# Further passes of the expert stage run as a pair's, on the weights that pass 11 left, and the pair that needs one changes places with pair 11

## The reference

```python
h = jax.nn.silu(jnp.einsum('td,edf->tef', xf, w_gate)) * jnp.einsum('td,edf->tef', xf, w_up)
h = h * gates.astype(h.dtype)[..., None]      # zero for all but the two chosen experts
y = jnp.einsum('tef,efd->td', h, w_down)
```

## Time and profile before

| what | us |
|---|---|
| median of three runs (622.78 to 623.87) | 623.35 |
| the profiled execution | 622.29 |
| its span, first instruction to last | 620.5 |
| PE busy in the span | 591.4 (95%) |
| VectorE busy | 321.1 (52%) |
| ScalarE busy | 232.6 (37%) |
| GpSimd busy | 53.0 (9%) |
| mean rate of all transfers | 259 GB/s |

### The profile page before, as it was taken

How to read it: one execution, slowest core, us unless ns; L and a number is a source line. 1 busy time by engine, 2 the same in 40 slices (tenths; PEclk the granted TensorE clock), 3 DMA queues, 4 the chain that set the end, 5 groups by cost and what they waited for, 6 DMA issues and landing times.

```text
span 620.5 us, 8828 instructions
## 1 busy us (share of the span) xinstructions
PE 591.4 (95%) x2860; PEld 352.3 (57%) x2860; DVE 321.1 (52%) x702; ACT 232.6 (37%) x413; POOL 53.0 (9%) x126
## 2 busy tenths in 40 slices
PE   7999999999999999999999989999999988988895
PEld 4876796777768677777566743433333333333331
DVE  4649787767767676776665876112111212211137
ACT  6451417375574747547364331111211121111124
POOL 1200001000000000000000012212121211121000
PEclk9999999999999999999999999999999999999999
DMA  8332319922222322221499879999999999999995
GB/s 318 128 135 88 118 34 359 387 77 76 74 69 101 109 68 76 76 84 52 178 343 419 306 274 376 412 419 419 417 420 419 423 418 421 420 417 422 413 386 211
DMA packets 34842, 160.78 MB, mean 259 GB/s; under 512 B 6528, under 2 KB 6912, under 8 KB 23040
## 3 DMA queue, kind: packets, MB, share of 16 engines
q1 hardware_dynamic: 29200, 149.66, 61.5%
q0 software_dynamic: 5472, 10.63, 4.6%
q10 hardware_dynamic: 144, 0.15, 0.1%
HBM read 155.01 MB, written 14.17 MB: 273 GB/s over the span
## 4 chain that ended last, share of the span: by engine, by line
PE 68%; SPq 11%; DMA 9%; DVE 6%; ACT 3%; issue 2%; DVEq 0%; ACTq 0%; POOLq 0%
PE ps L1617 14%; PE ps L1619 13%; PE ps L1618 13%; SPq L564 10%; PE ps L2026 10%; PE ps L2056 5%; DMA wslot<-in_wmoe 5%; PE ps L1758 2%; PE ps L1793 2%; DMA raw<-in_wmix 2%; DVE x L1570 1%; DMA ytok<-yo,idx 1%; PE ps L1740 1%; DMA gy<-ytok 1%; PE ps L1784 1%
## 5 line engine op out<-in xcount | busy, mean ns | idle before, releaser
L2026 PE MATMUL ps<-wslot,xgT 128*64 128x512 f32 x512 | 118.0, 594 | 7.8 <-DMA wslot<-in_wmoe 7.3
L1617 PE MATMUL ps<-xh,wh 128*128 128x512 f32 x256 | 102.5, 400 | 0.0
L1619 PE MATMUL ps<-xl,wh 128*128 128x512 f32 x256 | 99.9, 390 | 0.0
L1618 PE MATMUL ps<-xh,wl 128*128 128x512 f32 x256 | 99.9, 390 | 0.0
L757 ACT ACTIVATE wh<-raw 128x1024 fp32r<-128x1024 f32 x48 | 50.7, 1058 | 119.0 <-PE ps L1619 100.6
L2026 PEld LDWEIGHTS ps<-wslot,xgT 128*64 128x64 f32 x512 | 38.7, 137 | 82.0 <-issue 81.3
L1010 DVE TENSOR_TENSOR wl<-raw,wh 128x1024 fp32r<-128x1024 f32 x48 | 58.6, 1222 | 23.1 <-ACT wh L757 21.8
L2056 PE MATMUL ps<-wslot,hT 128*64 128x512 f32 x264 | 62.3, 598 | 4.2 <-ACT hT L968 2.2
L1523 DVE SCALAR_TENSOR_TENSOR hm<-ps,rt,hs 128x128 f32<-128x128 f32 x24 | 7.3, 345 | 112.9 <-ACT hs L965 112.9
L1617 PEld LDWEIGHTS ps<-xh,wh 128*128 128x128 f32 x256 | 48.1, 188 | 16.1 <-issue 6.7
L1619 PEld LDWEIGHTS ps<-xl,wh 128*128 128x128 f32 x256 | 48.1, 188 | 10.6
(11 more groups left out here) (356 smaller groups left out, 832.1 us busy)
## 6 DMA issues: line engine op xcount, KB each, us to landing
wslot<-in_wmoe SPq DMA_DIRECT2D x91, 1024.0 KB, 19.9
raw<-in_wmix SPq DMA_DIRECT2D x56, 512.0 KB, 4.0
wslot<-in_wmoe SPq DMA_DIRECT2D x8, 512.0 KB, 23.9
gy<-ytok SPq DMA_DIRECT2D x8, 512.0 KB, 10.3
xt<-in_x SPq DMA_DIRECT2D x4, 512.0 KB, 7.8
x<-in_x SPq DMA_DIRECT2D x4, 512.0 KB, 4.5
xnd<-x SPq DMA_DIRECT2D x4, 512.0 KB, 9.5
wslot<-in_wmoe SPq DMA_DIRECT2D x8, 256.0 KB, 4.8
```

The lines of the kernel that those rows point to most:

```text
L1617: pe.matmul(out, sh, mh_, start=start, stop=False)
L1618: pe.matmul(out, sl, mh_, start=False, stop=False)
L1619: return pe.matmul(out, sh, ml_, start=False, stop=stop)
L2026: l = pe.matmul(ps[CAP * s:CAP * s + CAP, 2, :], xgT[:, c, CAP * s:CAP * s + CAP], first_at[s * 4 + c] if first_at and c < 4 else wslot[q] ...
```

## The change

It does four things.

1. **A further pass is a pair's.** VectorE counts further passes by pair (the fuller expert decides), and the pass runs both halves (`pair(m + HEAD, 2, ...)`).
2. **It uses the weights in slot 2.** Pass 11's slot is slot 2 (KEPT = 11), and the first further pass needs no load if pass 11 was that pair's. If more than one is needed, or the pair could not be exchanged, the pair is loaded into slot 2.
3. **The pair that needs the first further pass (the last such pair, if it lies in 7 to 14, SWAP) changes places with pair 11.** VectorE writes the order of the pairs into nxi, SP reads from it which pair to load for passes 7 to 11 and places 12 to 14, and VectorE exchanges the columns of idx and rt (`swap_columns`); GpSimd and ScalarE wait for that (`swapped`).
4. **The slots behind it shift:** pairs 12, 13, 14, 15 use slots 0, 1, 2, 0. So gy, nf and junk3 move to where slot 1 lies, and yf to where slot 2 lies.

Of the diff, the parts that carry this:

```diff
+KEPT = HEAD - 1
+SWAP = range(7, PAIRS - 1)
+N_EXTRA, N_ORDER = 1, 1 + EXTRA
+N_NEED, N_COUNT, N_KEPT = N_ORDER + PAIRS, N_ORDER + PAIRS + 1, N_ORDER + PAIRS + 2
...
-    yf = at("yf", 122 * K, [P, TILES, D])
-
-    gy = at("gy", 48 * K, [P, 2, TILES, D])
-    nf = at("nf", 88 * K, [P, D])
-    junk3 = at("junk3", 92 * K, [P, D])
+    yf = at("yf", 48 * K, [P, TILES, D])
+
+    gy = at("gy", 98 * K, [P, 2, TILES, D])
+    nf = at("nf", 138 * K, [P, D])
+    junk3 = at("junk3", 142 * K, [P, D])
...
-            refill(1, 5, 14)
-            refill(2, 6, 16)
-            for q in range(3):
-                refill(q, 7 + q, 18 + 2 * q)
-
             e.wait_ge(nx_ready, 1)
             nx = e.value_load(nxi[0:1, 0:1], min_val=0, max_val=EXTRA)
 
+            def order(p):
+
+                return e.value_load(nxi[0:1, N_ORDER + p:N_ORDER + p + 1], min_val=0, max_val=NE - 2)
+
+            for p in range(7, 14):
+                refill(p % 3, p - 2, order(p))
+
             def further(count, m):
-                ex = e.value_load(nxi[0:1, bass.ds(m + 1, 1)], min_val=0, max_val=NE - 1)
-                for part, used in enumerate((gu_half, gu_mm, pair_mm)):
-                    lo, hi = PARTS[part]
-                    e.wait_ge(used, count)
-                    e.sem_inc(held, 1)
-                    e.dma_start(wslot[0][0][:, lo:hi], wmoe[bass.ds(ex, 1), :, lo:hi].rearrange(
-                        "a p c -> (a p) c")).then_inc(part_in[part][0][0], 16)
-
-            with e.If(nx > 0):
-                further(HEAD - 2, 0)
-            refill(1, HEAD - 1, 2 * HEAD)
-            refill(2, HEAD, 2 * HEAD + 2)
+
+                refill(2, count, e.value_load(nxi[0:1, bass.ds(m + N_EXTRA, 1)], min_val=0, max_val=NE - 2))
+
+            need = e.value_load(nxi[0:1, N_NEED:N_NEED + 1], min_val=0, max_val=1)
+            with e.If(need > 0):
+                further(HEAD, 0)
             with e.If(nx > 1):
                 with e.Fori(1, nx) as m:
                     further(m + HEAD, m)
-            refill(0, nx + HEAD, 2 * HEAD + 4)
+            refill(2, nx + HEAD, order(14))
...
-            with g.Fori(0, HEAD - 2) as G:
-                g.wait_ge(xgT_mm, FIRST + G + 2)
-                g.sem_inc(held, 1)
-                gather(idx, bass.ds(G + 2, 1), G + 2)
-                scatter(idx, bass.ds(G, 1), G + 1)
+            def rows_of_passes(a, b):
...
+            rows_of_passes(0, SWAP[0] - 2)
+            g.wait_ge(swapped, 1)
+            rows_of_passes(SWAP[0] - 2, HEAD - 2)
...
-            with a.Fori(1, HEAD) as G:
+            with a.Fori(1, SWAP[0]) as G:
+                expert_pass(G, rt[:, bass.ds(G, 1)])
+            a.wait_ge(swapped, 1)
+            with a.Fori(SWAP[0], HEAD) as G:
                 expert_pass(G, rt[:, bass.ds(G, 1)])
...
+                per = ps[:, TOTB, 0:NE].rearrange("p (e h) -> p e h", h=2)
...
+                own.then(d.reduce_max(most, per, axis=AX))
+                own.then(d.tensor_tensor(c8[:, 0:PAIRS, :], bc(most, nck), row(caps[:], PAIRS), ALU.is_gt))
+                own.then(d.reduce_sum(n, c8[:, 0:PAIRS, :], axis=AX))
+                own.then(d.tensor_tensor_scan(upto, ones[:, 0:PAIRS], n, 0.0, ALU.mult, ALU.add))
+                own.then(d.tensor_scalar(above, upto, -1.0, xcnt[:, 0, NE - 1:NE], ALU.mult, ALU.add))
...
+                own.then(d.tensor_scalar(one(0), pair1, float(SWAP[0] + 1), None, ALU.is_ge))
+                own.then(d.scalar_tensor_tensor(out=one(1), in0=pair1, scalar=float(SWAP[-1] + 1), in1=one(0), op0=ALU.is_le, op1=ALU.mult))
...
+                d.scalar_tensor_tensor(out=nxi[0:1, N_NEED:N_NEED + 1], in0=xcnt[0:1, 0, NE - 1:NE], scalar=1.0, in1=one(1),
+                                       op0=ALU.is_ge, op1=ALU.subtract)
...
+                own.then(d.tensor_tensor(moved, moved, iota[0:1, 0:PAIRS], ALU.add))
+                d.tensor_scalar(nxi[0:1, N_ORDER:N_ORDER + PAIRS], moved, 2.0, None, ALU.mult).then_inc(nx_ready, 1)
...
+            def swap_columns():
+
+                d.wait_ge(nx_ready, 1)
+                kept = d.value_load(nxi[0:1, N_KEPT:N_KEPT + 1], min_val=SWAP[0], max_val=SWAP[-1])
+                d.tensor_copy(turn[:, 0:2], idx[:, :, KEPT])
+                own.then(d.tensor_copy(turn[:, 2:3], rt[:, KEPT:KEPT + 1]))
+                d.tensor_copy(idx[:, :, KEPT:KEPT + 1], idx[:, :, bass.ds(kept, 1)])
+                own.then(d.tensor_copy(rt[:, KEPT:KEPT + 1], rt[:, bass.ds(kept, 1)]))
+                d.tensor_copy(idx[:, :, bass.ds(kept, 1)], turn[:, 0:2].rearrange("p (y a) -> p y a", a=1))
+                own.then(d.tensor_copy(rt[:, bass.ds(kept, 1)], turn[:, 2:3]))
+                d.sem_inc(swapped, 1)
...
             rows_T(2)
+            swap_columns()
             nx = extra_columns()
...
+            kept_in = pe.value_load(nxi[0:1, N_COUNT:N_COUNT + 1], min_val=use - 16, max_val=use)
             with pe.If(nx > 0):
                 with pe.Fori(0, nx) as m:
-                    pair(m + HEAD, 0, (m * 16 + use,), True, (m * 16 + (use - 16),))
-            pair(nx + HEAD, 1, (use, use), True)
-            pair(nx + (HEAD + 1), 2, (use, use), True)
+                    pair(m + HEAD, 2, (m * 16 + kept_in,) * 2, True)
+            pair(nx + HEAD, 0, (use, use), True, (use - 16, use - 16))
+            pair(nx + (HEAD + 1), 1, (use, use), True)
             pe.wait_ge(wlast_ready, 1)
             last_terms(0, ident[:], x1[:, 0, :], True, False)
-            pair(nx + (HEAD + 2), 0, (nx * 16 + use, use), True, (nx * 16 + (use - 16), use - 16))
-            pair(nx + (HEAD + 3), 1, (use + 16, use + 16), False)
+            pair(nx + (HEAD + 2), 2, (nx * 16 + kept_in,) * 2, True)
+            pair(nx + (HEAD + 3), 0, (use + 16, use + 16), False, (use, use))
```

More of the change, by code:

```diff
@@ L264, in build @@
     coly = small("coly", [P, 1], U32)
-    nxi = small("nxi", [1, 1 + EXTRA], I32)
+    nxi = small("nxi", [1, N_KEPT + 1], I32)
     warm = small("warm", [P, 1])
@@ L372, in build @@
         extra_ready = sem("extra_ready")
+        swapped = sem("swapped")
         colg_copied = sem("colg_copied")
@@ L726, in _ @@
             gather(idx, slice(1, 2), 1)
-            with g.Fori(0, HEAD - 2) as G:
-                g.wait_ge(xgT_mm, FIRST + G + 2)
-                g.sem_inc(held, 1)
-                gather(idx, bass.ds(G + 2, 1), G + 2)
-                scatter(idx, bass.ds(G, 1), G + 1)
+            def rows_of_passes(a, b):
+                with g.Fori(a, b) as G:
+                    g.wait_ge(xgT_mm, FIRST + G + 2)
+                    g.sem_inc(held, 1)
+                    gather(idx, bass.ds(G + 2, 1), G + 2)
+                    scatter(idx, bass.ds(G, 1), G + 1)
+            rows_of_passes(0, SWAP[0] - 2)
+            g.wait_ge(swapped, 1)
+            rows_of_passes(SWAP[0] - 2, HEAD - 2)
             g.wait_ge(extra_ready, 1)
@@ L1452, in extra_counts @@
                 d.wait_ge(total_mm, 1)
[L1453 to L1461, removed]
+                per = ps[:, TOTB, 0:NE].rearrange("p (e h) -> p e h", h=2)
+                most, n, upto, above = xcnt[:, 0, 0:PAIRS], xcnt[:, 1, 0:PAIRS], xcnt[:, 0, PAIRS:NE], xcnt[:, 1, PAIRS:NE]
@@ new lines, in extra_counts @@
+                one = lambda k: word[0:1, k:k + 1]
+                word = c8[0:1, PAIRS:NE, :].rearrange("p e c -> p (e c)")
+                own.then(d.reduce_max(most, per, axis=AX))
[3 more added lines that the diff above has]
+                own.then(d.tensor_scalar(above, upto, -1.0, xcnt[:, 0, NE - 1:NE], ALU.mult, ALU.add))
@@ new lines, in extra_counts @@
+                own.then(d.tensor_tensor(most, above, n, ALU.add))
+                own.then(d.tensor_copy(xcnt[:, 2, :].rearrange("p (e h) -> p e h", h=2), bc(above, 2)))
+                own.then(d.tensor_tensor(key17[0:1, :, 0:PAIRS], xcnt[0:1, 0:1, 0:PAIRS].broadcast_to([1, EXTRA, PAIRS]),
+                                         iota[0:1, 0:EXTRA].rearrange("p (m a) -> p m a", a=1).broadcast_to([1, EXTRA, PAIRS]), ALU.is_gt))
+                own.then(d.reduce_sum(cnt17[0:1, :], key17[0:1, :, 0:PAIRS], axis=AX))
@@ new lines, in extra_counts @@
+                pair1 = cnt17[0:1, 0:1]
+                d.tensor_copy(nxi[0:1, 0:1], xcnt[0:1, 0, NE - 1:NE])
+                d.tensor_scalar(word[0:1, 32:32 + EXTRA], cnt17[0:1, :], 2.0, -2.0, ALU.mult, ALU.add)
+                own.then(d.tensor_scalar(one(0), pair1, float(SWAP[0] + 1), None, ALU.is_ge))
+                own.then(d.scalar_tensor_tensor(out=one(1), in0=pair1, scalar=float(SWAP[-1] + 1), in1=one(0), op0=ALU.is_le, op1=ALU.mult))
+                own.then(d.scalar_tensor_tensor(out=one(2), in0=pair1, scalar=-float(KEPT + 1), in1=one(1), op0=ALU.add, op1=ALU.mult))
@@ new lines, in extra_counts @@
+                d.tensor_scalar(nxi[0:1, N_EXTRA:N_EXTRA + EXTRA], word[0:1, 32:32 + EXTRA], 0.0, None, ALU.max)
+                d.tensor_scalar(nxi[0:1, N_COUNT:N_COUNT + 1], one(1), -16.0, 16.0 * (HEAD // 3 + 1), ALU.mult, ALU.add)
```

(9 more changed lines are left out.)

10 lines of the change are left out of this document (5 added, 5 removed).

## The result

The changed kernel took 616.53 us in the median of 4 runs (615.48 to 617.03), before took 623.07 beside it (4 runs, 622.01 to 623.87). The ratio is 0.9896, with a 95% interval of 0.988 to 0.9912: 6.5 us faster. The forecast was 616.0, in a range of 614.9 to 619.4. The profiled execution took 616.25 us, its span is 614.6. Two later sets of runs gave the same median, 616.52 and 616.55 (6 runs each).

What follows compares the result with a forecast made beforehand. PE binds until pass 11, then PE and DMA nearly equally. 7.5 us of removed load less 0.2 at the end gives 7.3, other costs hidden: 616.0 us against the median, range 614.9 to 619.4.

Steps and rivals of the forecast that it cites:

- Does it take hold: One further pass runs, pair 14's; it follows pass 11 with weights still in slot 2; the exchange costs no bytes.
- Removed, 7.5 us of queue: One expert's three transfers (3.146 MB at 419 GB/s) go; everything from pair 12 on lands 7.5 us earlier.
- Both halves, +0.33: Further pass with 32 and 16 matmuls instead of 16 and 8: period 12.37 instead of 12.04 us, booked as +0.33.
- PE's new times: Passes 12.37 us apart after the further pass; all four weight waits go; place 14 ends 4.19 earlier, last half 6.67.
- The holds on slot 2, cost 0: Pair 14's loads wait for slot 2 about 1.5 us at issue; the deep queue hides it: cost 0, at most 1.5.
- SP, cost 0: Eight register loads of 0.50 us before refills, earlier wait for counts; hidden by queue depth: cost 0, at most 0.5.
- VectorE, hidden: 25 small operations for 8 before pass 0's gating end by 379.0, hidden by pass 0's matmuls; later column exchange 1.7 us.
- The end, 7.3: Read back's first piece follows the queue, 7.5 us earlier; 0.2 off for PE's last sums: gain 7.3 us.
- own range: Range of the main forecast itself, 615.2 to 617.2 us, for gains from 8.1 to 6.2 us; chance 0.73.
- The read back at 7.00 again: Rival at the end: the read back takes its 7.00 us again, only PE's 4.19 counts: 619.2 us; chance 0.13.
- Nothing gained: Rival: PE still waits at pairs 12 to 15, for slot 2's held loads or its own slowness: 623.4 us; chance 0.09.
- The slower rival: The exchange misses the pair, so the whole pair is loaded again, six transfers for three: +7.5 us, 630.9; chance 0.05.

Runs made afterwards that it cites:

- e5_fixed_order: Changed kernel with the exchange of pairs 11 and 14 written as constants, refills moved ahead of the wait for the counts: 616.84 us, ratio 0.9892 to before.
- e2_no_exchange: Changed kernel, but pair 14 may not change places, so the further pass loads its whole pair again: 648.14 us, ratio 1.039 to before.
- e6_extra_bytes: Changed kernel with two dummy transfers (1.84 MB) added ahead of the refill of place 12: 620.15 us, ratio 0.9944 to before.
- e8_short_pass: Changed kernel with the further pass taking four of its eight steps in gate and up (16 matmuls for 32): 616.76 us, ratio 0.989 to before.
- e9_same_bytes: Changed kernel with three dummy transfers putting back the removed 3.146 MB, ahead of places 12 and 13: 623.83 us, ratio 1.0005 to before.
- e3_sums_later: Changed kernel with the last tile's sums on PE moved from ahead of place 14 to behind it: 616.78 us, ratio 0.9894 to before.
- e7_order_end: Changed kernel with last tile's sums behind place 14, tile 2 read back before tile 0, tiles 1 and 2 combined earlier: 618.59 us, ratio 0.9913 to before.

## Why the prediction was right, step by step

- **Does it take hold.** Right: 32 matmuls in the further pass, three transfers fewer, and without the exchange 648 us.
- **Removed, 7.5 us of queue.** Right in rate and size. The rate was as in the earlier trace rows, 419 GB/s. With the load removed and nothing else the last weights land 7.61 and 7.58 us earlier than in before (588.84 and 588.87 for 596.45), and put back, the bytes bring back 623.8. In the changed kernel they land 6.67 and 6.81 earlier (589.78 and 589.64), in e5_fixed_order, without the register loads, 7.01 (589.44). The two traces without the load even start the stage 0.7 us later than before's. So the change itself seems to give back 0.8 to 0.9 us, some of it by the register loads or the wait ahead of them; this rests on one or two traces of each kernel, and where the rest comes from is open. It does not come from one place: after's landings are mostly about 0.5 later than before's from 386 to 471 us, up to 0.4 earlier from 483 to 500, and 0.3 to 0.6 later just ahead of the removed load.
- **Both halves, +0.33.** By starts, 528.19 to 540.61 is 12.42 us, before 12.04. But the 12.04 was misread: the group at 539.65 in the earlier trace rows holds only 31 matmuls, and the first of the 32 stands at 539.17. The transposes behind the two products tell it better. They are 546.98 - 534.62 = 12.36 us apart in before and 547.58 - 535.20 = 12.38 in after, and a full pair takes 12.37. The half pass already cost PE a whole one, so the right entry was 0. The half alone gave 616.44, and a saving of 3.4 us there brought nothing.
- **PE's new times.** Further pass 528.19 (said 527.61), pair 12 540.61 (539.98), pair 13 552.98 (552.35), place 14 567.36 (566.64), its end 576.30 + 3.65 = 579.95 (579.17), pair 15 579.78 (579.01), last half about 588.68 + 1.8 = 590.5 (589.92). All 0.6 to 0.8 late, of which 0.58 came with the start, out of the waits at the down products of passes 10 and 11 (1.07 and 0.72 in after, none in before). The prediction left pass 11's waits as they were. All four waits went, as said.
- **The holds on slot 2, cost 0.** Right: the share stays at 1.01 or above in every 5 us stretch from 528 to 585.
- **SP, cost 0.** Right for the kernel's time, at 0.28 us a load for the 0.50 taken; but see the waits at passes 10 and 11 above, which e5_fixed_order does not have.
- **VectorE, hidden.** The 25 operations ran from 371.37 to 376.30 (4.9 us, said 7.2 at most), and VectorE still waited for ScalarE:

```profile
376.14 0.16 DVE L1495 TENSOR_SCALAR nxi<-c 1x16 int32<-1x16 f32 x1
378.55 0.61 DVE L1569 SCALAR_TENSOR_TENSOR hm<-ps,rt,hs 128x128 f32<-128x128 f32 x2 [2.25 <-ACT hs L972]
```

- **The end, 7.3.** The mechanism was right: the read back's 7.00 us were not its own. Its first piece takes 3.4 to 3.7 us where the last weights land near its issue, 3.72 where they landed long before (e2_no_exchange), and 6.8, 6.8 and 6.3 where the queue was still full of weights at its issue (e6_extra_bytes, e8_short_pass, e9_same_bytes); e3_sums_later and e7_order_end lie between, with 5.1 and 5.5. In these five and in before it lands 2.9 to 3.6 us behind the last weights, whenever it was issued. The queue's end came out as said: stk landed at 591.46 (591.3 said, 598.82 before). Two sizes were off. The first piece came at 592.94 for 592.25: it was issued 0.85 later than said, as PE was late, and then took 3.53 us, which is about its own time without a queue. So it moved by 6.81 for 7.5. And a term was missing, that the pieces behind it might come later. VectorE's fourth step moved by 604.15 - 598.28 = 5.87, so 0.94 was lost behind the first piece, where 0.2 had been taken off for PE's last sums. In the profiled executions the gain is 622.29 - 616.25 = 6.04; in the medians 6.54. The own range of 615.2 to 617.2 holds the result because it was wide enough, not because it had counted these two losses.
- **The rivals.** The read back at 7.00 again (619.2) did not come true here, but 7 us is what a full queue brings, and it costs nothing extra there, since the queue's end is the bound. Nothing gained: excluded. The slower rival: real where the exchange is not possible, and 25 us instead of 7.5, because the order of the loads and the clock come on top of the bytes.

## What to carry to other kernels

Where PE waits for a full queue of transfers in several small pieces, price a change in bytes over the measured rate, and look at what must follow the queue: its latency in the trace may be half queueing, as here 7.00 us of which some 3.5 were its own. It moves with the queue's end until that time of its own, counted from its issue, becomes the later bound; so forecast both. Work added to an engine that only keeps pace with the queue is free up to the slack, and work taken from it brings nothing. When a load can be hoisted or moved behind others, price where it stands in the order, not only its size: e2_no_exchange loads 3 MB more than before, behind other loads, and took 25 us more, where the bytes alone would be 7.5.

## What the runs showed of the hardware

- A product on one half of the columns (16 matmuls, 7.08 us) takes as long as on both (32, 7.04 to 7.09 us), here shown by leaving a half out.
- PE stood still for 30.7 us in e2_no_exchange. The granted clock was 1.00 over 515 to 529 us, 0.68 over 529 to 535 and 0.50 (1.2 GHz) from 535 on. It stayed there through 559 to 564 us with PE at work; 564 to 570 had 0.89, then 1.00. The Trainium skill (TensorE: Matmul & The Clock Gate, What's actually happening) says that the idle state is throttled to half and that activity releases it; this trace agrees, and the product cost 9.83 - 7.09 = 2.7 us more.
- The queue of weights does not end sharply. In after the DMA share is 0.72, 0.60 and 0.34 in the three us from 586 to 589 and 0.15 in the next, while the last weights land at 589.78 and the read back is issued at 589.41. So about 1.5 of its first piece's 3.53 us pass with the DMA engines half idle or more:

```profile
589.00:590.00 1.00, 1.00 (x6) 0.29 (x4) 0.00 (x0) 0.00 (x0) 0.00 (x0) 1.00 0.15 58
590.00:591.00 1.00, 1.00 (x8) 0.41 (x6) 0.00 (x0) 0.00 (x0) 0.00 (x0) 1.00 0.51 119
591.00:592.00 1.00, 1.00 (x8) 0.17 (x4) 0.00 (x0) 0.00 (x0) 0.00 (x0) 1.00 0.88 356
```
